# Inverses of the gated delta rule: five of six doubling levels in packed 32x32 blocks on four row groups

## The chip, the cores and the metric

One core of a Trainium2 chip runs one program of about thirty stages. The metric is the device time of one execution in microseconds (us). The program's tiles stay in the core's SBUF and PSUM; weights come over DMA. TensorE (PE) multiplies, VectorE (DVE), ScalarE (ACT) and GpSimd (POOL) do the elementwise work.

## The reference, cut to what matters

The stage in question makes, for each of 8 heads and each of 8 chunks of 64 tokens, the inverse of a unit lower triangular 64x64 matrix, in float32:

```python
k_beta = k * beta[..., None]
lmat = jnp.where(strict, jnp.einsum('bhncd,bhnsd->bhncs', k_beta, k) * decay, 0.0)
eye = jnp.eye(CHUNK, dtype=jnp.float32)
t_inv = lax.linalg.triangular_solve(eye + lmat, jnp.broadcast_to(eye, lmat.shape),
                                    left_side=True, lower=True, unit_diagonal=True)
u = jnp.einsum('bhncs,bhnsd->bhncd', t_inv, v_beta)
w = jnp.einsum('bhncs,bhnsd->bhncd', t_inv, k_beta * jnp.exp(g)[..., None])
```

The kernel works on chunks of 128 tokens (two of the reference's chunks and the block that joins them), so that 4 chunks cover the 512 tokens, and inverts 128x128 unit triangular matrices.

## The kernel before, in words

`gdn_inverse` (L1216 to L1350) is one stage. `gdn_layer` calls it twice, for heads 0 to 3 and for heads 4 to 7; the four heads of a call are worked on side by side. Every stage ends in a barrier of all engines (L175), so nothing of the next stage runs beside it.

The inverse is built by doubling. A head's matrix is kept as two diagonal blocks of 64x64 per chunk, the upper one on partitions 0 to 63 (`low`) and the lower one on 64 to 127 (`high`): `am` holds the strict triangle, `pair` the inverse found so far (4 chunks x 64 columns) and its transpose (4 chunks x 64 columns more). Each of six levels doubles the size b of the inverted diagonal blocks, from 1 to 64, with T <- T - T (A masked) T, in five steps for each head i (n = 4*level + i counts them through):

1. POOL multiplies `am` by the level's mask into one of two buffers `part` (L1252, 128x256). From n = 2 on it waits until `u` of n-2 has been issued, since that frees the buffer.
2. PE makes `u` = masked A times T in PSUM: 8 matmuls of 64x64, alternating between the low and the high row group (L1276). It waits for the cut of n (and, from level 1 on, for the head's last update).
3. DVE scales `u` by beta into `prod` (L1323, 128x256).
4. PE makes `p`: 16 matmuls of 64x64 (L1288 for T's half, L1289 for the transposed half), chunk by chunk, low and high.
5. DVE subtracts `p` from `pair` (L1334, 128x512).

PE's order is written out: in each level `u` of the four heads, then `p` of the four heads. After six levels each 128x128 matrix lacks the block that joins its halves: one head after the other has 4+4 matmuls on one row group each (L1301, L1307), a scaling by DVE (L1323, 64x256) and a copy by ACT (L1349), and ACT copies the finished halves to the full matrices `inv_t` (L1346).

Beside that, the stage begins with DVE's four copies of the identity into `pair` (L1314, 128x512) and two large matmuls whose result nobody reads, which keep PE busy (L194, called by `keep_busy`), and POOL zeroes `inv_t` after its second cut (L1256, 128x2048), makes the scaled keys `kb` in the last levels (L1259, four of 128x512) and scales `k_tok` behind its last cut (L1263, four of 128x512). The masks of the levels lie in `gdn_masks`, 7 x 64 columns, loaded once in the program's first stage.

A float32 matmul of the code stands in the trace as two weight loads and two matmul records, four instructions of PE.

Of the kernel before, what the change touches and what calls it, by code (L numbers as in the profile page):

```python
# [26 lines left out]
P = 128  # L27
# [12 lines left out]
NCH = S // CH  # L40
LEVELS = 7
HB = CH // 2
HG = 4

FF_PART = 1408
# [1170 lines left out]
def gdn_inverse(prog, name, h0, beta, am, pair, inv_t, prod, part, k_tok, beG, kd, kb):  # L1216

    nc, ps = prog.nc, prog.ps
    DEEP = LEVELS - 1
    N = DEEP * HG
    W = NCH * HB
    low, high = slice(0, HB), slice(HB, P)

    def blocks(x):
        return x.rearrange("p (c n) -> p c n", n=HB)  # L1230

    def cut_of(c):
        return slice(c * HB, (c + 1) * HB)
    part = part[:, :, 0:W]
    hs = slice(h0 * P, (h0 + HG) * P)

    def heads(x):
        return x.rearrange("p (h n) -> p h n", n=P)
    eye = prog.level_masks[:, DEEP, :]
    with Stage(prog, name) as st:  # L1240
        start, cut, cleared = st.counter("start"), st.counter("cut"), st.counter("cleared")
        u_ready, u_copied = st.counter("u_ready"), st.counter("u_copied")
        p_ready, updated = st.counter("p_ready"), st.counter("updated")
        corner_ready, placed, keyed = st.counter("corner_ready"), st.counter("placed"), st.counter("keyed")

        @st.gpsimd
        def _(pool):
            for n in range(N):
                level, i = divmod(n, HG)
                if n >= 2:  # L1250
                    pool.wait_ge(u_ready, n - 1)
                nc.gpsimd.tensor_tensor(blocks(part[:, n % 2, :]), blocks(am[:, i, 0:W]),  # L1252
                                        prog.level_masks[:, level, :].unsqueeze(1).to_broadcast([P, NCH, HB]),
                                        ALU.mult).then_inc(cut, 1)
                if n == 1:
                    nc.gpsimd.memset(inv_t[:, :, :], 0.0).then_inc(cleared, 1)  # L1256
                if n >= N - 2 * NCH and n % 2:
                    c = (n - (N - 2 * NCH)) // 2
                    nc.gpsimd.tensor_tensor(heads(kb[:, c, :]), heads(k_tok[:, c, hs]),  # L1259
                                            beG[:, c, h0:h0 + HG].unsqueeze(2).to_broadcast([P, HG, P]), ALU.mult).then_inc(keyed, 1)  # L1260
            for c in range(NCH):
                pool.wait_ge(keyed, c + 1)
                nc.gpsimd.tensor_tensor(heads(k_tok[:, c, hs]), heads(k_tok[:, c, hs]),  # L1263
                                        kd[:, c, h0:h0 + HG].unsqueeze(2).to_broadcast([P, HG, P]), ALU.mult)

        @st.tensor
        def _(pe):
            def u(n):
                i = n % HG
                pe.wait_ge(cut, n + 1)  # L1270
                pe.wait_ge(start, min(n + 1, HG))
                if n >= HG:
                    pe.wait_ge(updated, n - HG + 1)
                for c in range(NCH):
                    for rows in (low, high):
                        m = nc.tensor.matmul(ps[rows, i, cut_of(c)], part[rows, n % 2, cut_of(c)],  # L1276
                                             pair[rows, i, cut_of(c)], start=True, stop=True)
                m.then_inc(u_ready, 1)

            def p(n):  # L1280
                i = n % HG
                pe.wait_ge(u_copied, n + 1)
                if n >= HG:
                    pe.wait_ge(updated, n - HG + 1)
# [8 lines left out]
            for level in range(DEEP):  # L1293
                for i in range(HG):
                    u(level * HG + i)
                for i in range(HG):
                    p(level * HG + i)
# [12 lines left out]

        @st.vector
        def _(dve):
            for i in range(HG):
                m = nc.vector.tensor_copy(blocks(pair[:, i, :]), eye.unsqueeze(1).to_broadcast([P, 2 * NCH, HB]))  # L1314
                m.then_inc(start, 1)

            def scaled(n, rows):
# [4 lines left out]
                scale = beta[rows, :, h0 + i:h0 + i + 1].to_broadcast([rows.stop - rows.start, NCH, HB])  # L1322
                nc.vector.tensor_tensor(blocks(prod[rows, i, 0:W]), blocks(ps[rows, i, 0:W]), scale, ALU.mult  # L1323
                                        ).then_inc(u_copied, 1)
            for level in range(DEEP):
                for i in range(HG):
                    scaled(level * HG + i, slice(0, P))
                for i in range(HG):
                    n = level * HG + i
                    dve.wait_ge(start, HG)  # L1330
                    if n >= HG:
                        dve.wait_ge(updated, n - HG + 1)
                    dve.wait_ge(p_ready, n + 1)
                    nc.vector.tensor_tensor(pair[:, i, :], pair[:, i, :], ps[:, HG + i, :], ALU.subtract).then_inc(updated, 1)  # L1334
            for i in range(HG):
                scaled(N + i, high)

        @st.scalar
        def _(act):
            def full(i, rows):  # L1340
                return inv_t[rows, i, :].rearrange("p (c n) -> p c n", n=P)
            act.wait_ge(cleared, 1)
# [265 lines left out]
def gdn_layer(prog, inp):  # L1608
    nc = prog.nc
    with ExitStack() as own:  # L1610
# [10 lines left out]
        masks = new("gdn_masks", [P, LEVELS * HB])  # L1621
        prog.level_masks = masks[:, :].rearrange("p (l n) -> p l n", n=HB)
        with ExitStack() as mid:
            q, k, z = (new(n, s, mid) for n, s in (("gdn_q", [P, HEADS, S]), ("gdn_k", [P, HEADS, S]), ("gdn_z", [P, NT, D])))
            with ExitStack() as before:
# [2 lines left out]
            with ExitStack() as early:  # L1628
# [2 lines left out]
                ba = new("gdn_ba", [P, NT, 2 * HEADS], early)  # L1631
                sums = new("gdn_sums", [P, NT * 2 * HEADS], early)
                first_stage(prog, inp, [(taps[:, :], inp["gdn_taps"]), (par[:, :], inp["gdn_par"]),
                                        (masks[:, :], inp["cst"][:, 3 * P:3 * P + LEVELS * HB])])
# [2941 lines left out]
def constants():  # L4576
# [3 lines left out]
    ones = np.ones((P, P))  # L4580
    tri = (i[:, None] <= i[None, :]) * 1.0
    levels = []
    s, c = i[:, None] % HB, i[None, 0:HB]
    for level in range(LEVELS - 1):
        b = 1 << level
        levels.append((s // (2 * b) == c // (2 * b)) & (s % (2 * b) < b) & (c % (2 * b) >= b))
    levels.append(s == c)
    return np.concatenate([ident, ones, tri] + [m * 1.0 for m in levels], axis=1).astype(np.float32)

# [87 lines left out]
```

## Time and profile before

| | |
|---|---|
| device time, median of 3 runs | 2674.49 us (2668.77 to 2674.54) |
| the profiled execution, its own time | 2675.39 us |
| its span in the trace | 2673.7 us |
| mean granted TensorE clock, share of full speed | 0.983 |
| PE busy over the span | 94% |
| first call of `gdn_inverse` | 244.0 to 290.5 us of the span |
| second call | 334.1 to 380.5 us |

### The profile page before, as it was taken

To read this page: it belongs to the slowest core of one execution; us is meant where nothing else is said; L and a number is where in the kernel's file an instruction comes from. 1 tells how busy PE (TensorE), PEld (TensorE's weight loads), DVE (VectorE), ACT (ScalarE), POOL (GpSimd) and SP (SyncE) were. 2 spreads that over 40 slices of the span, in tenths; PEclk is the share of its full clock that TensorE was granted. 3 is DMA by queue.
4 is the path that set the end of the run, shared out by engine and by line. 5 is a ranking of instruction groups with operands and counts; after the bars stand their busy time and mean duration, and the time that the engine had idled before them with its cause. 6 is when DMAs were issued, how large, how long until landed. Compare 5 with 4: busy or idle time off the path is not lost. (4 is left out here: it accounts for less than half of the span.)

```text
span 2673.7 us, 41986 instructions
## 1 busy us (share of the span) xinstructions
PE 2526.5 (94%) x16381; PEld 2079.4 (78%) x16381; DVE 1721.1 (64%) x2858; ACT 1032.3 (39%) x1475; POOL 545.4 (20%) x429
## 2 busy tenths in 40 slices
PE   8998989999999989899999999989998989999897
PEld 7887887788887769799999999957774666776466
DVE  6745666467667773667676667755785546677456
ACT  3341213421212342455555555513343443344353
POOL 1104441430320200234233334410110001020001
PEclk9999999999999999899999999999999999999999
DMA  4220001347653442367777767743220212222021
GB/s 150 91 83 33 2 3 63 129 151 249 199 190 119 132 108 64 123 224 251 233 234 251 237 228 245 264 135 93 77 81 27 85 56 78 90 83 66 27 79 63
DMA packets 262241, 340.80 MB, mean 127 GB/s; under 512 B 24960, under 2 KB 220032, under 8 KB 261504
## 3 DMA queue, kind: packets, MB, share of 16 engines
q1 hardware_dynamic: 253888, 315.52, 36.4%
q0 software_dynamic: 4736, 16.78, 1.8%
q10 hardware_dynamic: 3456, 6.29, 0.8%
q8 instruction: 109, 1.79, 0.3%
q14 instruction: 52, 0.43, 0.1%
HBM read 318.63 MB, written 17.30 MB: 126 GB/s over the span
## 5 line engine op out<-in xcount | busy, mean ns | idle before, releaser
L2946 PE MATMUL ps<-x_feat_r,moe_w_hi 128*128 128x384 f32 x1408 | 405.1, 359 | 1.0 <-DVE x_feat_r L3046 1.0
L2511 DVE TENSOR_TENSOR moe_w_lo<-ring,moe_w_hi 128x2048 fp32r<-128x2048 f32 x144 | 315.8, 2193 | 118.8 <-ACT moe_w_hi L2506 118.8
L2949 PE MATMUL ps<-x_feat_r,moe_w_lo 128*128 128x192 f32 x1408 | 354.5, 252 | 0.0
L2506 ACT ACTIVATE moe_w_hi<-ring 128x2048 fp32r<-128x2048 f32 x144 | 254.8, 1770 | 93.0 <-PE ps L263 75.5
L2949 PEld LDWEIGHTS ps<-x_feat_r,moe_w_lo 128*128 128x128 f32 x1408 | 268.8, 191 | 0.3
L2946 PEld LDWEIGHTS ps<-x_feat_r,moe_w_hi 128*128 128x128 f32 x1408 | 264.3, 188 | 1.9 <-issue 1.6
L267 PE MATMUL ps<-x_free_r,ring_r 128*128 128x512 f32 x496 | 196.5, 396 | 0.0
L266 PE MATMUL ps<-ring_r,x_feat_r 128*128 128x256 f32 (+2 forms) x576 | 186.3, 323 | 0.0
L194 PE MATMUL ps<-cst 128*128 128x384 f32 x326 | 125.8, 538 | 21.0 <-PEq L175 19.0
L263 PE MATMUL ps<-x_feat_r,ffn_w_hi 128*128 128x512 f32 x352 | 139.3, 396 | 1.2 <-DVE ffn_w_lo L2454 1.2
L267 PE MATMUL ps<-x_feat_r,ffn_w_lo 128*128 128x512 f32 x352 | 139.4, 396 | 0.0
L266 PE MATMUL ps<-x_free_r,ffn_w_hi 128*128 128x512 f32 x352 | 138.5, 393 | 0.0
L2506 ACT ACTIVATE ffn_w_hi<-ring 128x2048 fp32r<-128x2048 f32 (+1 forms) x35 | 61.8, 1768 | 170.1 <-PE ps L263 101.0
L3854 ACT ACTIVATE s_sb<-s_sb,att_small 128x512 f32<-128x512 f32 (+3 forms) x128 | 71.8, 561 | 140.7 <-DVE att_small L3846 140.3
L266 PEld LDWEIGHTS ps<-ring_r,x_feat_r 128*128 128x128 f32 x576 | 110.5, 192 | 8.7 <-issue 0.6
L194 PEld LDWEIGHTS ps<-cst 128*128 128x128 f32 x326 | 65.6, 209 | 66.2 <-issue 34.8
L267 PEld LDWEIGHTS ps<-x_free_r,ring_r 128*128 128x128 f32 x496 | 93.7, 189 | 21.1
L3843 DVE CUSTOM_DVE_ANT_0 s_sb<-ps,tables 128x128 f32<-128x128 f32 (+3 forms) x104 | 49.3, 474 | 94.0 <-PE ps L3793 75.2
L3861 ACT ACTIVATE p_t<-ps 128x512 f32<-128x512 f32 (+3 forms) x128 | 55.1, 431 | 132.0 <-PE ps L3793 132.0
L263 PE MATMUL ps<-x_feat_r,acc_r 128*128 128x512 f32 x256 | 102.3, 400 | 0.0
L2993 ACT ACTIVATE moe_cross<-ps 128x384 f32<-128x384 f32 (+1 forms) x96 | 44.4, 463 | 148.2 <-PE ps L2949 148.2
L267 PE MATMUL ps<-x_feat_r,ring_r 128*128 128x512 f32 x256 | 101.1, 395 | 0.0
(619 smaller groups left out, 6455.3 us busy)
## 6 DMA issues: line engine op xcount, KB each, us to landing
ring<-in_moe_w SPq DMA_DIRECT2D x120, 1024.0 KB, 5.3
ring<-in_w_in SPq DMA_DIRECT2D x32, 1024.0 KB, 5.3
ring<-in_ffn_w SPq DMA_DIRECT2D x30, 1024.0 KB, 7.6
ring<-in_ada_t SPq DMA_DIRECT2D x48, 512.0 KB, 4.0
ring<-in_gdn_w_in SPq DMA_DIRECT2D x12, 1024.0 KB, 5.7
ring<-in_moe_w SPq DMA_DIRECT2D x24, 512.0 KB, 3.7
ring<-in_s_w_glu SPq DMA_DIRECT2D x8, 1024.0 KB, 5.6
ring<-in_w_out SPq DMA_DIRECT2D x8, 1024.0 KB, 6.4
```

Of the source, the lines that this page charges most:

```text
L194: prog.nc.tensor.matmul(prog.ps[:, bank, 0:3 * P], prog.ident, prog.cst, start=True, stop=True)
L263: m = nc.tensor.matmul(out, lh, rh, start=first, stop=False)
L266: nc.tensor.matmul(out, lh, rl, start=False, stop=False)
L267: return nc.tensor.matmul(out, ll, rh, start=False, stop=last)
L2506: self.prog.nc.scalar.activation(self.flat(self.hi, j % SPLITS, j), self.raw(j), ACT.Copy).then_inc(self.hi_done, 1)
L2511: self.prog.nc.vector.tensor_tensor(self.flat(self.lo, j % SPLITS, j), self.raw(j), self.flat(self.hi, j % SPLITS, j).bitcast(F32), ALU.su ...
L2946: mm = nc.tensor.matmul(out, wh[:, k, cs], both[:, k, :], start=(k == 0), stop=False)
L2949: mm = nc.tensor.matmul(out[:, 0:SLOTS], wl[:, k, cs], xg[0][:, k, :], start=False, stop=(k == KD - 1))
L2993: nc.scalar.activation(cross_of(c, which), half(c, which, 1), ACT.Copy).then_inc(cross_copied, 1)
L3843: self.nc.vector.tensor_tensor_reduce(out=x, in0=scores, in1=table, scale=1.0, scalar=-3.0e38, op0=ALU.add, op1=ALU.max, accum_out=mx).the ...
L3854: self.nc.scalar.activation(x, x, ACT.Exp, bias=self.small[:, u % 4, 1:2], scale=self.heads[h][3], accum_out=self.small[:, u % 4, 2:3]).th ...
L3861: self.nc.scalar.activation(self.p_t[:, u % 2, 0:self.keys(u)], self.ps[:, 2 + u % 2, 0:self.keys(u)], ACT.Copy).then_inc(self.pt_copied, 1)
```

## The change

Levels 0 to 4 now work on 32x32 blocks. For them the chunk's four 32x32 diagonal blocks lie on four row groups (partitions 0 to 31, 32 to 63, ...), and a head's operands are packed to 4 chunks x 32 columns:

- `am_small` is `am` without the columns that belong to the other block of a pair, packed at the stage's start by two copies on ACT (L1415) and two on DVE (L1362), 32x4x128 each. POOL waits for all four.
- A level's `u` is 16 matmuls of 32x32 for a head (L1293), its `p` 32 (L1306, L1309), four row groups in turn. DVE scales 128x128 (L1370) and subtracts 128x256 (L1386) for a head, POOL's cut is 128x128 (L1274).
- Level 0 multiplies by the identity from the mask table instead of `pair`; `p` there is 16 matmuls for a head, and DVE makes both halves of the pair as identity minus a product (L1379, L1381). The four copies L1314 are gone.
- After level 4 the pair is widened to the old form for the last level: two copies on DVE (L1391, L1392) and two on ACT (L1426, L1427) for a head, 32x8x32 each, into `pair`, which POOL has zeroed after its fourth cut (L1281). The last level (L1321, L1331, L1332) waits for them (`wide_act`, `wide_dve`); it and the joining blocks (L1348, L1354) are as before.
- The key scalings leave POOL and stand on ACT, 16 + 16 instructions of 128x128 (L1411). ACT also zeroes the lower left blocks of `inv_t` (L1419, four of 64x256) in place of POOL's memset of the whole.
- The mask table is 256 columns in place of 448. The stage's semaphore counters are 14 in place of 10.

In matmuls of the code a call has 608 before (24 x 8 for `u`, 24 x 16 for `p`, 32 at the end), and 1024 after (128 in level 0, 192 in each of levels 1 to 4, 96 in the last level, 32 at the end).

```diff
+            pool.wait_ge(packed_act, 2)
+            pool.wait_ge(packed_dve, 2)
             for n in range(N):
                 level, i = divmod(n, HG)
                 if n >= 2:
                     pool.wait_ge(u_ready, n - 1)
...
+                if n < NQ:
+                    nc.gpsimd.tensor_tensor(blocks(part[:, n % 2, 0:QW], QB), blocks(am_small[:, i, :], QB),
+                                            prog.quarter_masks[:, level, :].unsqueeze(1).to_broadcast([P, NCH, QB]),
+                                            ALU.mult).then_inc(cut, 1)
...
+            def u_quarters(n):
+                i = n % HG
+                pe.wait_ge(cut, n + 1)
+                if n >= HG:
+                    pe.wait_ge(updated, n - HG + 1)
+                for c in range(NCH):
+                    cs = cut_of(c, QB)
+                    for rows in quarters:
+                        m = nc.tensor.matmul(ps[rows, i, cs], part[rows, n % 2, cs],
+                                             pair_small[rows, i, cs] if n >= HG else eye[rows], start=True, stop=True)
+                m.then_inc(u_ready, 1)
+
+            def p_quarters(n):
...
+                for c in range(NCH):
+                    cs, ts = cut_of(c, QB), cut_of(NCH + c, QB)
+                    if n >= HG:
+                        for rows in quarters:
+                            nc.tensor.matmul(ps[rows, HG + i, cs], pair_small[rows, i, ts], u_small[rows, i, cs],
+                                             start=True, stop=True)
+                    for rows in quarters:
+                        m = nc.tensor.matmul(ps[rows, HG + i, ts], u_small[rows, i, cs],
+                                             pair_small[rows, i, ts] if n >= HG else eye[rows], start=True, stop=True)
+                m.then_inc(p_ready, 1)
...
-            for i in range(HG):
-                m = nc.vector.tensor_copy(blocks(pair[:, i, :]), eye.unsqueeze(1).to_broadcast([P, 2 * NCH, HB]))
-                m.then_inc(start, 1)
...
+                    if level == Q_LEVELS - 1:
+                        dve.wait_ge(updated, n + 1)
+                        dve.wait_ge(emptied, 1)
+                        nc.vector.tensor_copy(*widen(i, 2))
+                        nc.vector.tensor_copy(*widen(i, 3)).then_inc(wide_dve, 1)
```

What it does to the order of the engines, at three places. PE's own list, the first two levels of a call, before (one of its four heads' `p`, each row a matmul of the code or several alike):

```order
L194 MATMUL ps<-cst 128x384 x2
L1276 MATMUL ps<-gdn_inv,gdn_sq 64x64 x32
L1288 MATMUL ps<-x_feat,gdn_inv 64x64
L1289 MATMUL ps<-gdn_inv,x_feat 64x64
L1288 MATMUL ps<-x_feat,gdn_inv 64x64
L1289 MATMUL ps<-gdn_inv,x_feat 64x64
```

and the same place after:

```order
L197 MATMUL ps<-cst 128x384 x2
L1293 MATMUL ps<-gdn_masks,gdn_sq 32x32 x64
L1309 MATMUL ps<-gdn_masks,x_feat 32x32 x64
L1293 MATMUL ps<-x_feat,gdn_sq 32x32 x64
L1306 MATMUL ps<-x_feat 32x32 x4
L1309 MATMUL ps<-x_feat 32x32 x4
```

The order of `u` and `p` is kept; a level has twice as many matmuls, of a quarter of the block each, and level 0 has no L1306.

DVE's list around the last two levels of a call, where `x_feat` is the packed `prod` and `gdn_inv` the `pair`, before (three last levels, and the scalings at the end):

```order
L1323 TENSOR_TENSOR x_feat<-ps,gdn_small 128x256 x4
L1334 TENSOR_TENSOR gdn_inv<-gdn_inv,ps 128x512 x4
L1323 TENSOR_TENSOR x_feat<-ps,gdn_small 128x256 x4
L1334 TENSOR_TENSOR gdn_inv<-gdn_inv,ps 128x512 x4
L1323 TENSOR_TENSOR x_feat<-ps,gdn_small 64x256 x4
```

and after (level 4 with one head's widening, of which four stand there, and the last level):

```order
L1370 TENSOR_TENSOR x_feat<-ps,gdn_small 128x128 x4
L1386 TENSOR_TENSOR x_feat<-x_feat,ps 128x256
L1391 COPY gdn_inv<-x_feat 32x8x32
L1392 COPY gdn_inv<-x_feat 32x8x32
L1386 TENSOR_TENSOR x_feat<-x_feat,ps 128x256
...
L1370 TENSOR_TENSOR x_feat<-ps,gdn_small 128x256 x4
L1399 TENSOR_TENSOR gdn_inv<-gdn_inv,ps 128x512 x4
```

The copies stand between the subtractions of level 4, ahead of the last level's scalings.

POOL's list of a call, before:

```order
L1252 TENSOR_TENSOR gdn_sq<-x_free,gdn_masks 128x256 x2
L1256 MEMSET x_free 128x2048
L1252 TENSOR_TENSOR gdn_sq<-x_free,gdn_masks 128x256 x16
L1259 TENSOR_TENSOR acc<-gdn_ktok,gdn_small 128x512
L1252 TENSOR_TENSOR gdn_sq<-x_free,gdn_masks 128x256 x2
```

and after:

```order
L1274 TENSOR_TENSOR gdn_sq<-x_feat,gdn_masks 128x128 x4
L1281 MEMSET gdn_inv 128x2048
L1274 TENSOR_TENSOR gdn_sq<-x_feat,gdn_masks 128x128 x16
L1278 TENSOR_TENSOR gdn_sq<-x_free,gdn_masks 128x256 x4
```

The memset has moved from behind the second cut to behind the fourth, the cuts are half as wide, and no key scaling is left.

## Rows read from the trace of the kernel before

**Rows 1.** The span by stretches of stages: length, busy time with records, clock, DMA.
```profile
core 0: us, PE busy (x) PEld busy (x) DVE busy (x) ACT busy (x) POOL busy (x), PEclk, DMA share, GB/s
244.00:292.00 48.00, 44.84 (x1232) 41.44 (x1233) 31.57 (x57) 4.83 (x12) 26.88 (x33) 0.96 0.02 4
334.00:382.00 48.00, 43.19 (x1233) 40.58 (x1234) 32.02 (x57) 4.83 (x12) 27.14 (x33) 1.00 0.02 4
```

**Rows 2.** Marks in time of the first call: barrier, first u, first corner block.
```profile
L175 PEldq EVENT_SEMAPHORE x2: 51/51/51, 244.0 to 290.5; - x2
...
L1276 PE MATMUL ps<-gdn_inv,gdn_sq x384: 218/218/366, 246.9 to 282.5; 64*64 64x64 f32 x192
...
L1301 PE MATMUL ps<-gdn_inv,x_free x32: 218/218/267, 286.1 to 288.0; 64*64 64x64 f32 x32
```

**Rows 3.** Groups of instructions in 244 to 292: count, busy us, mean ns, idle before.
```profile
L1252 POOL TENSOR_TENSOR gdn_sq<-x_free,gdn_masks 128x256 f32<-128x256 f32 x24 | 17.2, 737 | 16.4 <-PE ps L1276 15.5 <-POOLq L175 0.3
L1334 DVE TENSOR_TENSOR gdn_inv<-gdn_inv,ps 128x512 f32<-128x512 f32 x24 | 16.5, 687 | 8.3 <-PE ps L1289 8.3
L1276 PE MATMUL ps<-gdn_inv,gdn_sq 64*64 64x64 f32 x384 | 15.6, 226 | 2.4 <-POOL gdn_sq L1252 2.3
L1323 DVE TENSOR_TENSOR x_feat<-ps,gdn_small 128x256 f32<-128x256 f32 x24 | 9.7, 420 | 5.0 <-PE ps L1276 5.0
L1259 POOL TENSOR_TENSOR acc<-gdn_ktok,gdn_small 128x512 f32<-128x512 f32 x4 | 4.2, 1040 | 0.0
L1346 ACT ACTIVATE x_free<-gdn_inv 64x256 f32<-64x256 f32 x8 | 3.3, 415 | 43.7 <-DVE gdn_inv L1334 43.5
```

**Rows 4.** One level of the first call, by stretches: its p phase, its u phase.
```profile
256.60:260.34 3.74, 3.74 (x135) 3.74 (x133) 2.34 (x5) 0.00 (x0) 1.04 (x2) 1.00 0.02 4
260.34:263.08 2.74, 2.34 (x72) 2.07 (x70) 1.93 (x5) 0.00 (x0) 1.78 (x3) 1.00 0.00 0
```

**Rows 5.** Records on one row group alone, and L2322's first loads after idle time.
```profile
L1307 PE MATMUL ps<-gdn_inv,x_feat x32: 218/218/267, 287.8 to 289.7; 64*64 64x64 f32 x32
...
961.60:961.64 0.04, 0.01 (x1) 0.04 (x2) 0.50 0.00 0
```

**Rows 6.** DMA queues in 244 to 290, and in 250.2 to 253.8 with its 40 slices.
```profile
q8 instruction: 10, 0.16, 1.5%
...
DMA  0700000000000000000000000000000000000007
q8 instruction: 2, 0.03, 3.8%
```

**Rows 7.** A far jump of PE's sequencer, then DMA in 1762.5:1765.1, 1765.1:1765.8, 1765.8:1767.
```profile
L3220 PEldq COMPARE_BRANCH  x2: 89/1829/3569, 1109.1 to 1761.5; - x2
...
q8 instruction: 1, 0.02, 3.0%
...
DMA packets 0, 0.00 MB, mean 0 GB/s; under 512 B 0, under 2 KB 0, under 8 KB 0
...
q8 instruction: 1, 0.02, 5.0%
```

**Rows 8.** Stretches ahead of a lower granted clock, and at it (columns as in rows 1).
```profile
224.30:227.70 3.40, 1.47 (x14) 1.24 (x13) 1.30 (x4) 1.91 (x4) 1.95 (x2) 0.99 0.00 0
227.70:231.10 3.40, 3.40 (x18) 3.40 (x18) 3.24 (x8) 0.29 (x1) 2.86 (x2) 0.51 0.02 5
237.90:241.30 3.40, 1.16 (x9) 0.86 (x8) 1.18 (x3) 2.20 (x4) 2.35 (x2) 1.00 0.01 2
241.30:244.70 3.40, 0.62 (x1) 0.50 (x2) 2.80 (x6) 0.00 (x0) 3.08 (x3) 0.50 0.00 0
```

**Rows 9.** Nearest rows for the new small operations, from other stages of the program.
```profile
L3861 ACT ACTIVATE p_t<-ps 128x128 f32<-128x128 f32 x32 | 8.7, 272 | 29.2 <-PE ps L3793 29.2
L3854 ACT ACTIVATE s_sb<-s_sb,att_small 128x128 f32<-128x128 f32 x32 | 12.8, 401 | 29.8 <-DVE att_small L3846 29.6
L3874 DVE COPY acc<-ps 128x128 f32<-128x128 f32 x64 | 18.2, 284 | 10.9 <-PE ps L3808 10.9
```

More of the change, by code:

```diff
@@ L1223, in gdn_inverse, with blocks, cut_of, side @@
     nc, ps = prog.nc, prog.ps
-    DEEP = LEVELS - 1
-    N = DEEP * HG
-    W = NCH * HB
+    N = (Q_LEVELS + 1) * HG
+    NQ = Q_LEVELS * HG
+    W, QW = NCH * HB, NCH * QB
     low, high = slice(0, HB), slice(HB, P)
[L1229 to L1233, printed above, removed]
+    quarters = [slice(r * QB, (r + 1) * QB) for r in range(P // QB)]
+    def blocks(x, n=HB):
+        return x.rearrange("p (c n) -> p c n", n=n)
+    def cut_of(c, n=HB):
+        return slice(c * n, (c + 1) * n)
+    def side(r):
+        return slice((r % 2) * QB, (r % 2 + 1) * QB)
     part = part[:, :, 0:W]
     hs = slice(h0 * P, (h0 + HG) * P)
+    u_small, am_small, pair_small = prod[:, :, 0:QW], prod[:, :, QW:2 * QW], prod[:, :, 2 * QW:4 * QW]
     def heads(x):
         return x.rearrange("p (h n) -> p h n", n=P)
-    eye = prog.level_masks[:, DEEP, :]
+    eye = prog.quarter_masks[:, Q_LEVELS, :]
     with Stage(prog, name) as st:
-        start, cut, cleared = st.counter("start"), st.counter("cut"), st.counter("cleared")
+        cut, cleared, emptied = st.counter("cut"), st.counter("cleared"), st.counter("emptied")
+        packed_act, packed_dve = st.counter("packed_act"), st.counter("packed_dve")
+        wide_act, wide_dve = st.counter("wide_act"), st.counter("wide_dve")
         u_ready, u_copied = st.counter("u_ready"), st.counter("u_copied")
@@ L1251, in _ @@
                     pool.wait_ge(u_ready, n - 1)
[L1252 to L1264, printed above, removed]
+                if n < NQ:
+                    nc.gpsimd.tensor_tensor(blocks(part[:, n % 2, 0:QW], QB), blocks(am_small[:, i, :], QB),
+                                            prog.quarter_masks[:, level, :].unsqueeze(1).to_broadcast([P, NCH, QB]),
+                                            ALU.mult).then_inc(cut, 1)
+                else:
+                    nc.gpsimd.tensor_tensor(blocks(part[:, n % 2, :]), blocks(am[:, i, 0:W]),
+                                            prog.half_mask.unsqueeze(1).to_broadcast([P, NCH, HB]), ALU.mult).then_inc(cut, 1)
@@ L1292, in _ @@
             keep_busy(prog, 2 * HG - 1, 2)
-            for level in range(DEEP):
+            for level in range(Q_LEVELS):
                 for i in range(HG):
-                    u(level * HG + i)
+                    u_quarters(level * HG + i)
                 for i in range(HG):
-                    p(level * HG + i)
+                    p_quarters(level * HG + i)
+            for i in range(HG):
+                u(NQ + i)
+            for i in range(HG):
+                p(NQ + i)
             for i in range(HG):
@@ L1312, in _, with scaled @@
         def _(dve):
-            for i in range(HG):
-                m = nc.vector.tensor_copy(blocks(pair[:, i, :]), eye.unsqueeze(1).to_broadcast([P, 2 * NCH, HB]))
-                m.then_inc(start, 1)
-            def scaled(n, rows):
+            eyes = eye.unsqueeze(1).to_broadcast([P, NCH, QB])
+            for r in (2, 3):
+                nc.vector.tensor_copy(*pack(r)).then_inc(packed_dve, 1)
+            def scaled(n, rows, width=HB):
                 i = n % HG
@@ L1321, in scaled @@
                     dve.wait_ge(p_ready, n - HG + 1)
[L1322 to L1325, printed above, removed]
+                scale = beta[rows, :, h0 + i:h0 + i + 1].to_broadcast([rows.stop - rows.start, NCH, width])
+                nc.vector.tensor_tensor(blocks(prod[rows, i, 0:NCH * width], width), blocks(ps[rows, i, 0:NCH * width], width),
+                                        scale, ALU.mult).then_inc(u_copied, 1)
@@ L1335, in _ @@
+            for i in range(HG):
+                scaled(NQ + i, slice(0, P))
+            for i in range(HG):
+                dve.wait_ge(wide_act, i + 1)
+                dve.wait_ge(wide_dve, i + 1)
+                dve.wait_ge(p_ready, NQ + i + 1)
+                nc.vector.tensor_tensor(pair[:, i, :], pair[:, i, :], ps[:, HG + i, :], ALU.subtract).then_inc(updated, 1)
             for i in range(HG):
@@ L1341, in full, with scale_keys @@
                 return inv_t[rows, i, :].rearrange("p (c n) -> p c n", n=P)
+            def scale_keys(dst, factor):
+                for c in range(NCH):
+                    for h in range(HG):
+                        m = nc.scalar.activation(heads(dst[:, c])[:, h, :], heads(k_tok[:, c, hs])[:, h, :], ACT.Copy,
+                                                 scale=factor[:, c, h0 + h:h0 + h + 1])
+                return m
+            for r in (0, 1):
+                nc.scalar.activation(*pack(r), ACT.Copy).then_inc(packed_act, 1)
+            scale_keys(kb, beG).then_inc(keyed, 1)
+            nothing = prog.ones[high, 0:1].unsqueeze(2).to_broadcast([HB, NCH, HB])
+            for i in range(HG):
+                m = nc.scalar.activation(full(i, high)[:, :, low], nothing, ACT.Copy, scale=0.0)
+            m.then_inc(cleared, 1)
+            act.wait_ge(keyed, 1)
+            scale_keys(k_tok[:, :, hs], kd)
+            act.wait_ge(emptied, 1)
+            for i in range(HG):
+                act.wait_ge(updated, NQ - HG + i + 1)
+                nc.scalar.activation(*widen(i, 0), ACT.Copy)
+                nc.scalar.activation(*widen(i, 1), ACT.Copy).then_inc(wide_act, 1)
             act.wait_ge(cleared, 1)
@@ L4582, in constants @@
     levels = []
-    s, c = i[:, None] % HB, i[None, 0:HB]
-    for level in range(LEVELS - 1):
+    s, c = i[:, None] % QB, i[None, 0:QB]
+    for level in range(Q_LEVELS):
         b = 1 << level
```

50 lines of the change are left out of this document (37 added, 13 removed).

## Prediction

> **What bounds the kernel now.** I read the busy shares by stretches first. The two calls of the stage take 46.4 us each (barrier at 244.0, next at 290.5 [rows 2]), together 3.5% of the span; PE is busy for 93% and 90% of them, DVE for some 66%, and DMA moves next to nothing (share 0.02) [rows 1]. No transfer runs underneath that a shorter stage would expose, and each stage ends in a barrier, so what the stage gains or loses I pass on whole, twice. The profiled execution took 2675.39 us against a median of 2674.49; I add differences to the median.
>
> Inside a call, the marks in time give three parts [rows 2]: 2.9 us until the first u, 39.2 us of six levels, 4.4 us of corner blocks. One level is 3.74 us of p, in which PE is never idle, and 2.74 us of u, in which PE waits for POOL's cuts [rows 4]; 6.48 us together. A float32 matmul of the code is four PE instructions, so p's 64 matmuls in 3.74 us are 58.4 ns each, 29.2 ns per matmul record, 14.6 ns per instruction. One row group alone takes 1.9 us for 31 intervals of a record, 61 ns each [rows 5]: two row groups really ran side by side, and the rate of p is that of the array. That is what the change attacks.
>
> **The change, part by part.** I divide a call after the change into a fixed part and Q, the time of the five narrow levels.
>
> Start. POOL's first cut now waits for packing. The nearest row for the copy is ACT at 415 ns for 64x256 [rows 3]; for twice the columns I take 0.6, then about 0.35 to hand over, 0.45 for a cut of half the elements of the 737 ns one [rows 3], and the rest of the start-up: 1.75 us until the first u, in place of 2.9. (In the second call it was 1.5; I keep 1.75 for both.)
>
> Last level: 6.5 us as a level of before [rows 4]. Corner: 4.3. Widening: DVE has two copies more for each head between subtractions. The bounds are 284 ns (a 128x128 copy [rows 9]) and ACT's 415 [rows 3]; four heads are about 2.2 us more on DVE, of which the next head's p hides most. I charge 1.0 us, with 0 to 2.5 as the ends. Fixed part: 1.75 + 1.0 + 6.5 + 4.3 = 13.55 us. The call breaks even at Q = 46.35 − 13.55 = 32.8 us.
>
> Moved off POOL: 8.2 us of key scalings (L1259 four times 1.04, and four like it) [rows 3]. They lay in POOL's gaps or behind its last cut; on ACT they are 32 instructions of 272 to 401 ns [rows 9], 9 to 13 us, where ACT was idle for 43.7 us [rows 3]. Widening is wanted some 25 us or more after the start, so I cost this at nothing; without that cover it would be those 9 to 13 us. The memset behind cut 3 is 1.8 us of POOL in a level whose cuts have shrunk to about 0.45; it may hold up level 1's first cuts by about a microsecond, once. POOL's waits (2.3 us of PE's idle time [rows 3]) shrink with the cuts. The shorter mask table belongs to the program's first stage and is hidden: nothing.
>
> Q, if PE and DVE alone decide. A level has 192 matmuls of 32x32 on four row groups. If a group needs about as long as it does for 64 columns now (61 ns per record at the most [rows 5], half of that with the half-wide block), a matmul costs 61/4, about 15.6 ns, and a level 3.0 us of PE. DVE then has four scalings and four subtractions of half the size (9.7 us and 16.5 us for 24 of each now [rows 3], so 2.2 us a level at half the elements), with the latency from PE to DVE and back at both seams: 3.7 us a level. Level 0 has 128 matmuls and eight instructions on DVE, 3.8. Q = 3.8 + 4 x 3.7 = 18.6, and a call takes 32.2, 14.2 us less.
>
> But PE has to get its instructions. A narrow level is 768 of them, and a block of 256 would be used up in 1.0 us. On the instruction queue there are 10 packets of 16 KB in 46 us [rows 6], and PE had about 2465 records in the stage [rows 1], so one packet is 256 instructions. They come one at a time: two within 250.2 to 253.8, one at either end, and none between [rows 6], 3.5 us apart, just as fast as PE uses them up. A packet takes 16 x 46 x 1.5% / 10 = 1.10 us. How far ahead is it asked for? The far jump at 1761.5 shows it [rows 7]: the branch lasts 3.57 us, until 1765.07; the target's packet takes 1.25 us of it (3.0% of 16 x 2.6); from 1765.1 to 1765.8 no packet of any kind moves; at 1765.8, 0.75 us after PE went on, the next block's packet begins. So the next block is asked for when the engine enters the one ahead of it, and not before. From entering a block to being able to enter the next it takes L = 0.75 + 1.10, and what it takes from the packet's end until its instructions can be used. The jump shows 1.3 us for that. The ends: 1.85 us (nothing behind the packet) and 3.4 (the whole branch, less the longer packet: 3.57 − 1.25 + 1.10). I take 3.15, since only the jump shows the steps one by one. Before, a block lasted at least 3.74 us in the p phase, so none of this could be seen.
>
> The narrow levels have 128 + 4 x 192 = 896 matmuls, 3584 instructions, 14 blocks. The first is there; 13 are waited for: Q = 1.0 + 13 x 3.15 = 42.0. A call takes 55.5 us, 9.2 more than now; two calls **+18.3 us**. At L = 1.85 it would be Q = 25.1, 38.6 us, −15.4 for both; at 3.4, +24.8; the change breaks even at L = 2.45.
>
> The page "Runtime: NRT & Kernel Launch" of the Trainium skill, section Instruction fetch mechanics, also has blocks of 256 instructions, the next fetched while the current one runs, and calls crossing into one "mostly hidden". With that in the narrow levels the call would take the 32.2 us worked out above; the trace agrees on the size of a block, and is silent on whether one of 1.0 us can hide a packet.
>
> **Clock.** A PE that works 1.0 us in 3.15 is idle for most of the time. The granted clock fell to 0.50 behind stretches with PE busy for 1.47 and 1.16 of 3.4 us, and stayed there for at least 3.4 us [rows 8]. While PE waits for instructions that costs nothing; at the entry into the last level, 3.4 us of work at half clock lose 1.7 us. Twice: +3.4. With it 2674.5 + 18.3 + 3.4 = 2696; since it may have risen again by then, I write 2695.
>
> **The rivals.**
> (1) *Fetch is hidden* (more than one block ahead once the stream is sequential). Then Q is set by PE and DVE: 18.6 us, total −28.4, 2646; if the front of PE is slower than the array, less is won. After idle time the next load followed within 40 ns of the first [rows 5]; taken as the price of a matmul's four instructions, 896 of them are 35.8 us, with 1 us of waits Q = 36.8, +8. The case spans 2646 to 2682, the low end likelier, since that row is a bound from above. For it: nothing before ever ran short. Against it: the 0.7 us without a packet after the jump [rows 7].
> (2) *Fetch binds, but quicker*: L from 1.85 to 2.6. 2659 to 2678.
> (3) *Slower by issue, whatever is fetched*: PE never got past one matmul record in 29.2 ns or an instruction in 14.6 ns [rows 4]. If that is the limit of the front and not of the array, a level is 192 x 58.4 = 11.2 us and level 0 7.5: Q = 52.4, 66 us a call, +39 in all, 2714. It turns the sum from about 35.5 ns a matmul on (31.8 us over 896). Against it: one row group alone takes 61 ns per record [rows 5], two together half of that, as an array limit would have it.
> The page "TensorE: Matmul & The Clock Gate", section Wait — 56ns, not 53.3ns?, has start-to-start never under about 25 ns, however small the matmul. Taken across row groups, two records a matmul, that is an estimate of 50 ns, 9.6 us a level, Q = 45, +24; the 29.2 ns of rows 4 do not contradict it.
> (4) *The change doesn't do what it says*: were the four groups not run side by side, a level would be as in (3) or worse; it goes into its chance.
>
> **How the numbers follow.** Forecast (fetch-bound, L 2.6 to 3.4): 0.40, 2679 to 2704. Rival 1: 0.27. Rival 2: 0.18. Rivals 3 and 4: 0.15, 2698 to 2714. What a measurement of this kernel can tell from no change is 0.3%, 8 us. Faster by more: four fifths of rival 1 and half of rival 2, 0.31. Within: the rest of both, and a tenth of the forecast (its short end), 0.18. Slower by more: 0.51. The range leaves the fastest end of rival 1 and the upper end of rival 3 out: 2650 to 2706.
>
> **What would show it.** In the trace of after: packets on the instruction queue in the narrow levels at a steady distance L whatever PE does, with all engines idle between the end of one block's work and the next; the first u at about 1.75 us; a narrow level of 9 to 10 us; the clock at 0.50 in places; DVE's share of the stage down. If packets come 1.0 to 1.3 us apart, rival 1 holds; if PE's records are evenly spaced by about 29 ns through the narrow levels, rival 3. My forecast falls if more than one block is in store.

## The result, and the profile after

The changed kernel takes 2714.8 us (median of 4 runs, 2714.1 to 2715.5) against 2674.5 us (2668.8 to 2678.6): a ratio of 1.0147, 95% interval 1.0135 to 1.0159, 40.3 us more. The forecast was 2695 us, range 2650 to 2706: the sign was right, the size half of what came. All times in this document are of fast runs alone, which leaves out one of five runs of the kernel called "both" below, at 4937 us.

All of it lies in the two calls. First the barriers at either end of both, then both calls by stretch (length, busy time with records of PE, PEld, DVE, ACT, POOL, the granted clock, DMA share), of the changed kernel:

```profile
L178 PEldq EVENT_SEMAPHORE  x2: 51/51/51, 246.2 to 312.8; - x2
L178 PEldq EVENT_SEMAPHORE  x2: 51/51/51, 356.4 to 422.4; - x2
...
246.15:312.83 66.68, 41.45 (x2052) 37.01 (x2052) 22.91 (x66) 20.30 (x58) 13.54 (x25) 0.61 0.02 4
356.36:422.39 66.03, 41.10 (x2052) 36.58 (x2052) 23.17 (x66) 20.30 (x58) 13.53 (x25) 0.61 0.02 4
```

A call was 46.4 us [rows 2] and is 66.7 and 66.0 now: 40 us together. PE has 820 records more on either side than before [rows 1], and yet is busy for fewer microseconds: 41.5 of 66.7 in the first call. DVE and POOL, most of whose instructions were halved in size, are busy for less as well. By the records of all engines, none of them works for 27% of the first call and 24% of the second, and for a third of the narrow levels. The granted clock, 0.96 and 1.00 before, is 0.61.

What ended PE's idle time, from the groups of instructions in 244 to 310 (busy us, mean ns, then the idle time ahead and its releaser):

```profile
L1309 PE MATMUL ps<-x_feat 32*32 32x32 f32 x512 | 15.8, 236 | 7.2 <-issue 7.2
L1306 PE MATMUL ps<-x_feat 32*32 32x32 f32 x512 | 15.7, 236 | 7.3 <-issue 7.3
L1293 PE MATMUL ps<-x_feat,gdn_sq 32*32 32x32 f32 x512 | 9.0, 226 | 8.6 <-issue 7.8 <-POOL gdn_sq L1274 0.8
```

"issue" is time in which the engine waited for nothing that the profile shows: no semaphore, no other engine. The three rows have 22.3 us of it together. Before, no row of this stage had more than 1.1 us of it in the levels; the idle time of L1276 was POOL's [rows 3].

What it was stands in four stretches of level 1 and the start of level 2 (in pairs: PE working, PE stopped), and in the DMA of 261 to 268 (40 slices of 0.175 us):

```profile
260.00:261.75 1.75, 1.72 (x127) 1.71 (x127) 0.74 (x2) 0.00 (x0) 0.00 (x0) 0.50 0.03 9
261.75:264.00 2.25, 0.23 (x16) 0.10 (x8) 0.10 (x1) 0.00 (x0) 0.00 (x0) 0.50 0.00 0
264.00:265.75 1.75, 1.73 (x127) 1.73 (x126) 0.75 (x2) 0.00 (x0) 0.00 (x0) 0.50 0.04 9
265.75:267.85 2.10, 0.19 (x14) 0.06 (x5) 0.32 (x2) 0.00 (x0) 0.45 (x1) 0.50 0.00 0
...
DMA  0000300000000000000000004000000000000000
q8 instruction: 2, 0.03, 2.0%
```

PE runs 127 matmul records and as many loads, one block of 256 instructions, in 1.75 us; then hardly anything runs on the whole core for 2.1 to 2.3 us, and the next 127 follow. The packet with the next block starts at 261.7 and 265.3, near the end of each burst (a burst is such a run of 256 instructions), and the burst that it feeds begins 2.3 to 2.6 us later. Over the narrow levels it goes on like that:

```profile
DMA packets 13, 0.21 MB, mean 4 GB/s; under 512 B 0, under 2 KB 0, under 8 KB 0
q8 instruction: 13, 0.21, 2.0%
```

13 packets in 250 to 300, 3.83 us apart in the mean, 3.45 to 4.12 each; a packet itself takes 16 x 50 x 2.0% / 13 = 1.2 us.

The last level, its u and its p:

```profile
300.50:304.40 3.90, 3.79 (x68) 3.53 (x65) 2.61 (x8) 1.43 (x4) 1.54 (x2) 0.50 0.02 4
304.40:308.40 4.00, 4.00 (x128) 4.00 (x126) 2.10 (x4) 1.08 (x3) 0.00 (x0) 0.89 0.03 6
```

7.9 us against the 6.48 of [rows 4]: u at half clock, p at nearly full.

### The profile page after: what moved, and what is told of

It is laid out like the page before. It is cut to its first block and busy times, and to the rows that moved or that the text cites. A ratio compares the mean times of both kernels' runs of the same rounds, so it can differ in the third digit from the quotient of the medians.

```text
span 2713.8 us, 45414 instructions
## 1 busy us (share of the span) xinstructions
PE 2522.2 (93%) x18045; PEld 2071.8 (76%) x18045; DVE 1703.8 (63%) x2878; ACT 1063.5 (39%) x1567; POOL 518.3 (19%) x413
## 5 line engine op out<-in xcount | busy, mean ns | idle before, releaser
L197 PEld LDWEIGHTS ps<-cst 128*128 128x128 f32 x326 | 64.2, 205 | 64.0 <-issue 31.8
```

The source lines that it names most:

```text
L197: prog.nc.tensor.matmul(prog.ps[:, bank, 0:3 * P], prog.ident, prog.cst, start=True, stop=True)
```

## The experiments

### Ten stages of PE work alone

Two explanations give almost the same time for this kernel: waiting for blocks of instructions (13 x 3.8 us), and a PE that cannot issue faster than 14.6 ns per instruction (rival 3, which came out at 2714). The trace shows bursts, which speak for the first; this kernel holds everything else away.

```diff
+def probe(prog, name, size, groups, n, loop):
+    rows = [slice(r * size, (r + 1) * size) for r in range(groups)]
+    def work(count):
+        for j in range(count // groups):
+            bank, at = (j // 2) % 7, (j % 2) * P
+            for r in rows:
+                nc.tensor.matmul(ps[r, bank, at:at + n], prog.ident[r, 0:size], prog.cst[r, 0:n], start=True, stop=True)
...
+            if loop:
+                with pe.Fori(0, loop):
+                    work(64)
+            else:
+                work(384)
```

> The kernel before with ten more stages ahead of the first call of gdn_inverse, each with PE work alone, whose results nobody reads: 384 matmuls written out (stages a, b, c: 32x32 blocks on four row groups with 32, 64, 128 moving columns; h: 64x64 blocks on two row groups with 64 columns) or a loop of 12 rounds of 64 matmuls (d, e, f: as a, b, c; g: as h; i and j: 32x32 blocks with 32 columns on one and on two row groups). Each starts with the same 12 large matmuls. Fetch theory (a block of 256 PE instructions follows the one ahead by about 3.9 us at the least, as the trace of the changed kernel has it): a, b and c take the same time, six blocks of 3.9 us, some 23 us, whatever the columns; d, the same matmuls twice over in a loop that fetches nothing after its first round, takes 768 times 15 to 27 ns, 12 to 21 us, and e and f take more with the columns. Issue theory (PE takes about 15 ns for each of its instructions, four a matmul): a takes 384 x 58 ns = 22 us as well, but d takes 768 x 58 ns = 45 us. g should take 58.4 ns a matmul in both, 45 us, and h 22 us: there no fetch shows. i tells what one row group takes: if d's time a matmul is a quarter of it, the array sets d.

The ten stretches a to j, in order (length first; a matmul of the code is two records):

```profile
256.65:275.98 19.33, 10.20 (x769) 9.55 (x768) 0.00 (x0) 0.00 (x0) 0.00 (x0) 0.61 0.02 5
287.26:306.01 18.75, 11.83 (x769) 11.19 (x768) 0.00 (x0) 0.00 (x0) 0.00 (x0) 0.98 0.02 4
317.67:339.81 22.14, 21.70 (x768) 20.89 (x768) 0.00 (x0) 0.00 (x0) 0.00 (x0) 1.00 0.01 4
348.73:365.27 16.54, 15.24 (x1536) 14.01 (x1536) 0.00 (x0) 0.00 (x0) 0.00 (x0) 1.00 0.00 1
374.17:397.37 23.20, 23.20 (x1537) 21.88 (x1536) 0.00 (x0) 0.00 (x0) 0.00 (x0) 1.00 0.00 1
406.23:448.09 41.86, 41.86 (x1537) 41.85 (x1536) 0.00 (x0) 0.00 (x0) 0.00 (x0) 1.00 0.00 0
457.01:501.80 44.79, 44.79 (x1536) 44.79 (x1536) 0.00 (x0) 0.00 (x0) 0.00 (x0) 1.00 0.00 0
510.67:533.07 22.40, 22.40 (x769) 22.40 (x768) 0.00 (x0) 0.00 (x0) 0.00 (x0) 1.00 0.01 4
541.93:619.88 77.95, 77.95 (x1536) 77.95 (x1536) 0.00 (x0) 0.00 (x0) 0.00 (x0) 0.54 0.00 0
631.59:656.94 25.35, 25.35 (x1537) 25.15 (x1536) 0.00 (x0) 0.00 (x0) 0.00 (x0) 1.00 0.00 1
```

a and d are the same matmul, 32x32 with 32 columns on four row groups. Written out, 384 of them take 19.3 us, 50.3 ns each, with PE busy for half of it; in a loop, 768 take 16.5 us, 21.5 ns each. So PE issues an instruction in 5.4 ns or less: rival 3 has fallen, and so has the prediction's estimate of 50 ns for a matmul. Written out, twice the columns (b) cost nothing, 18.8 us (b began with more of its list at hand, 526 records ahead of its first stop against 324 in a, but its bursts lie 3.7 to 4.0 us apart and those of a 3.5 to 3.7), and four times the columns (c) 3 us more than a; in a loop the same steps cost 16.5, 23.2 and 41.9 us (21.5, 30.2, 54.5 ns a matmul). The 64x64 form takes 58.3 ns whether written out (h) or in a loop (g): 256 of its instructions last 3.7 us, and a packet is on its way meanwhile. Six blocks had been expected to take some 23 us; a and b took 19, since only four or five of their blocks were waited for. The packets of a lay 3.33 to 3.79 us apart (mean 3.62, at a clock of 0.61), those of b 3.49 to 4.12 (mean 3.82, at 0.98): the interval is no shorter at the higher clock.

What several row groups bring has to be compared at one clock. Stage i, on one row group, ran at full clock only at its start; the granted clock then fell to 0.50, though PE was never idle in it:

```profile
541.93:545.00 3.07, 3.07 (x98) 3.07 (x98) 0.00 (x0) 0.00 (x0) 0.00 (x0) 1.00 0.02 5
550.00:560.00 10.00, 10.00 (x192) 10.00 (x191) 0.00 (x0) 0.00 (x0) 0.00 (x0) 0.50 0.00 0
```

At 1.00 its matmul records start 31.8 ns apart, 64 ns a matmul; two row groups (j) take 33.0 and four (d) 21.5. So the second row group halves the time and the third and fourth together take another third off. A quarter of one group's time would be 16 ns; what keeps four groups at 21.5 stays open.

### The narrow levels in a loop

If the waits are for fetching, PE's list must be shortened without taking a matmul away. In this kernel the five narrow levels are five rounds of one loop on PE; the other engines are as in the changed kernel, but for level 0, which is like the others and has 64 matmuls more.

```diff
-            for level in range(Q_LEVELS):
+            with pe.Fori(0, Q_LEVELS) as e:
                 for i in range(HG):
-                    u_quarters(level * HG + i)
+                    u_quarters(i, e)
                 for i in range(HG):
-                    p_quarters(level * HG + i)
+                    p_quarters(i, e)
...
+            def gate(i):
+                nc.tensor.matmul(ps[0:HB, i, BANK - 1:BANK], prog.ident[0:QB, 0:HB], prog.cst[0:QB, 0:1], start=True, stop=True)
```

> The changed kernel with its five narrow levels on PE in a hardware loop of five rounds, so that their 768 instructions are fetched once and not five times. Level 0 is then like the others (192 matmuls, the pair begins as copies of the identity), and ahead of each head's u and p stands one matmul with a single moving column that carries the wait. Matmuls of the narrow levels: 960 + 40 in place of 896. Fetch theory: three blocks of 3.9 us once, then four levels at PE's own rate (15 to 27 ns a matmul, 3.7 to 6 us a level): Q of 27 to 36 us in place of 52, so 32 to 50 us less in all than the changed kernel, 2665 to 2683 us. Issue theory (58 ns a matmul): no gain, 2715 us or a little more.

2702.0 us (ratio to before 1.0109, 1.0092 to 1.0126): 13 us less than the changed kernel, not 32 to 50. The fetching did go, and something else took its place. Two levels of it:

```profile
265.00:274.00 9.00, 8.81 (x420) 8.14 (x412) 2.85 (x8) 0.00 (x0) 1.81 (x4) 0.50 0.00 0
274.00:283.00 9.00, 8.77 (x416) 8.10 (x412) 2.85 (x8) 0.00 (x0) 1.81 (x4) 0.50 0.00 0
```

PE is busy for 98% of it, and a level takes 9.0 us. The cost was my own gate: a head's 16 matmuls of u took 0.42 us, and the next head's began 0.88 us after the first of them, so a gate took 0.46 us at half clock, and a level has eight. So the gate was put on PE's sequencer:

```diff
             def gate(i):
-                nc.tensor.matmul(ps[0:HB, i, BANK - 1:BANK], prog.ident[0:QB, 0:HB], prog.cst[0:QB, 0:1], start=True, stop=True)
+                pe.sem_inc(passed, 1)
```

> As loop5 (the five narrow levels in a hardware loop on PE), but the eight waits of a level stand on a semaphore instruction of PE's sequencer in place of a small matmul over two column groups. In loop5 four heads' u started 0.88 us apart with 0.42 us of matmuls in each, at half clock. If those matmuls were what ate the gain, a level goes from 9.0 us to 5.0 + the two seams between PE and DVE of 0.5 us, some 6 us at half clock and 4.5 at full clock: 11.7 + 4 x 6 = 36 us for the narrow levels, 50 to 53 us a call in place of 60, 2681 to 2687 us. If the levels are held up by something else (PE to DVE and back, POOL), it stays near 2700.

2672.4 us (median of 10; ratio to before 0.9988, 0.9979 to 0.9997), 9 us below the range expected. The first four of the five levels, in order:

```profile
247.43:256.06 8.63, 4.71 (x385) 4.26 (x385) 2.67 (x8) 8.58 (x30) 3.45 (x5) 0.90 0.02 6
256.06:262.09 6.03, 5.57 (x384) 5.37 (x385) 2.67 (x9) 0.76 (x3) 1.75 (x4) 0.50 0.00 0
262.09:267.02 4.93, 4.14 (x384) 3.94 (x385) 3.05 (x9) 0.00 (x0) 1.74 (x4) 0.95 0.00 0
267.02:271.75 4.73, 4.04 (x385) 3.84 (x385) 2.81 (x9) 0.00 (x0) 1.74 (x4) 1.00 0.00 0
...
q8 instruction: 3, 0.05, 0.6%
```

Three packets in 247 to 276, where the changed kernel has 13 in 247 to 300. The first round waits for its blocks (8.6 us), the second takes 6.0 us at half clock, the later ones 4.7 to 4.9 us at full clock, for 192 matmuls. Against the changed kernel's 11.5 us a level (three blocks of 3.83) even the round at half clock is half as long, so it was the fetching and not the clock that made the level long. With the fetching of four rounds taken away, 64 matmuls a call more and the clock that came with it, the kernel is 42 us faster than the changed one, more than the whole loss against before. The clock rose at the third level. That PE ran without long gaps by then isn't the whole reason: in the kernel with the small matmuls PE was busy for 98% of these levels and the clock stayed at 0.50 through all of them. What raises it isn't shown.

### Filling PE to hold the clock

```diff
                 pe.sem_inc(passed, 1)
+                if i == 0:
+                    nc.tensor.matmul(ps[:, i, BANK // 2:BANK], prog.ident, prog.cst[:, 0:BANK // 2], start=True, stop=True)
```

> As loop5e with one 128x128 matmul of 256 columns ahead of each level's u and each level's p, whose result nobody reads: ten a call, 0.3 us each at full clock, 3 us a call. If the low granted clock of the narrow levels comes from PE doing too little in them, these keep it at 1.00, a matmul of a narrow level costs 16 to 21 ns in place of 26, and a level 4.5 us; 48 us a call, 2677 us. If the clock stays at 0.50, they cost 5 us a call and the time is 10 us above that of loop5e.

2682.3 us, 10 us above loop5e. It reads like the case in which the clock stays low, but it isn't: here are 30 us of either call.

```profile
250.00:280.00 30.00, 24.45 (x1553) 20.01 (x1551) 11.13 (x32) 6.10 (x20) 8.02 (x18) 0.83 0.00 1
350.00:380.00 30.00, 25.09 (x1588) 20.60 (x1588) 12.60 (x37) 4.31 (x14) 7.50 (x16) 0.83 0.00 1
```

The rounds at full clock start 6.1 us apart in place of 4.7 to 4.9: a filler costs some 0.65 us, not 0.3. That is its own work: like every float32 matmul it is two matmul records, here 0.32 us apart, and the packed matmuls go on 0.31 us after the second. I had priced one record for two. The run therefore says nothing about what a steady clock would be worth.

### Two narrow levels in place of five

```diff
-Q_LEVELS = LEVELS - 2
+Q_LEVELS = 2
+WIDE_LEVELS = LEVELS - 1 - Q_LEVELS
```

with the masks of the other four levels in 64x64 form, and these levels run in it.

> The changed kernel with two narrow levels in place of five; levels 2 to 5 run in 64x64 blocks as before, and widening stands behind level 1. Fetch or issue theory alike: a narrow level is three blocks of 3.9 us, 11.7 to 11.9 us, a wide one 6.5; three levels fewer in the narrow form are 3 x 5.3 = 16 us a call less, 32 in all, 2683 us. If it were instead something that comes once in a call (the packing, the widening, the clock at the end), the time would stay within 5 us of 2715.

2683.8 us (1.0031, 1.0018 to 1.0044), as forecast to the microsecond: 31 us less than the changed kernel for three levels fewer in each of two calls, 5.2 us a level. Both explanations had forecast this, so it doesn't part them. The loss is a price per narrow level; packing, widening and the start can hold a few microseconds of it at most.

### The key scalings back on POOL

The changed kernel, with L1411's 32 instructions gone from ACT and the four plus four of before on POOL again.

> The changed kernel with one part undone: the key scalings are on POOL again, between the last eight cuts and behind them. The prediction costed the move at nothing. PE waits 2 us and more for each block of instructions in levels 3 and 4, so POOL's four operations of 1.04 us there are covered; in the last level PE is the slower. Expected: 2715 us, within 3. If POOL's scalings were on the path, up to 4 us a call more, 2723.

2708.7 us, under the 2712 to 2718 expected, but its four runs spread over 2702.7 to 2715.6. It isn't slower than the changed kernel (2714.1 to 2715.5), so moving the keys had brought nothing that shows. Whether it is faster isn't settled: the ratios to before, 1.0137 (1.0120 to 1.0154) and 1.0147 (1.0135 to 1.0159), overlap. Its profiled run was its fastest, with a span 13 us shorter than that of the changed kernel's profiled run, and only 3.8 us of them lie within the two calls. The packets lay 3.70 and 3.77 us apart in its two calls, against 3.83 and 3.76, which explains 1.5 us.

### The good parts without the narrow blocks

Two things in the stage need no 32x32 block: level 0 from the identity (a part of the change), and PE's waits for POOL's cuts [rows 3, 4], which four buffers end (2.3 us of PE's idle time in the first call before, none with four buffers). `part` is twice as wide as its two buffers, so the room is there.

```diff
-    part = part[:, :, 0:W]
+    part = part.rearrange("p b (a n) -> p (b a) n", n=W)
...
-                if n >= 2:
-                    pool.wait_ge(u_ready, n - 1)
+                if n >= HG:
+                    pool.wait_ge(u_ready, n - HG + 1)
...
-                                             pair[rows, i, cut_of(c)], start=True, stop=True)
+                                             pair[rows, i, cut_of(c)] if n >= HG else eye[rows], start=True, stop=True)
```

Both together:

> The kernel before, in 64x64 blocks throughout, with two parts of its own: level 0 multiplies by the identity from the mask table and leaves out its product for the first half (32 matmuls fewer, no copies of the identity at the start), and POOL's cuts go through four buffers in place of two. In level 0 1.9 us of p go, and up to 1.5 us of the start; the waits of PE for POOL's cuts, 0.9 us in each of five levels, go as well: 6 to 7 us a call less than before, 2661 to 2663 us. If the waits for POOL only move to another place, half of that, 2668.

Both, with the key scalings on ACT:

> As wide_both (64x64 blocks, first level from the identity, four buffers for the cuts), with the key scalings moved from POOL to ACT as in the changed kernel and POOL's memset behind the fourth cut. POOL's 1.04 us operations between the last cuts held nobody up once the cuts ran ahead by four buffers: no change against wide_both, 2665 us, within 2 us. If they still delayed cuts, up to 1 us a call less. Against the kernel before: 9 us less, 0.3 to 0.4%.

Level 0 from the identity alone:

> The kernel before with one part of the change alone, in 64x64 blocks: level 0 multiplies by the identity from the mask table, leaves out the product for the first half (32 matmuls of 58.4 ns, 1.9 us) and the copies of the identity at the start. The last of these held PE up in both calls (first u at 2.9 and 1.5 us, second head's at 4.9 and 3.8 us). Expected 2 to 3.5 us a call less, 2667 to 2670 us. If the waits for POOL's cuts take the gain away, 1 us a call, 2672.

Four buffers alone:

> The kernel before with four buffers for POOL's cuts in place of two, and nothing else. PE's waits for the cuts, 0.9 us in each of five levels, go, and POOL's 24 cuts of 0.74 us (18 us a call) stay below PE's time: 3 to 4.5 us a call less, 2666 to 2669 us. The two single changes together should come to the 9 us of the combined kernel.

| kernel | us | ratio to before, 95% |
|---|---|---|
| level 0 from the identity alone | 2668.3 | 0.9982 (0.9971 to 0.9994) |
| four buffers alone | 2667.2 | 0.9971 (0.9959 to 0.9982) |
| both | 2663.4 | 0.9954 (0.9938 to 0.9970) |
| both, key scalings on ACT | 2661.4 | 0.9957 (0.9945 to 0.9969) |

The last two are one result by their ratios. The barriers of a call of the third, and the first call of the fourth by stretch:

```profile
L175 PEldq EVENT_SEMAPHORE  x2: 51/51/51, 243.9 to 285.7; - x2
...
244.38:285.92 41.54, 40.26 (x1156) 37.52 (x1156) 27.80 (x56) 14.40 (x44) 19.14 (x25) 0.96 0.02 4
```

41.8 and 41.5 us for a call in place of 46.4, PE busy for 97% of the latter. Both beat the kernel before and the changed one, by 0.4% and by 2%. Each single change came in within its expectation; the two gains add up, 0.18% and 0.29% alone and 0.46% together, at the short end of what was expected.

With the waits for POOL gone, blocks of instructions begin to be waited for in the 64x64 form too. With four buffers alone, first call:

```profile
PEld ps L1288 <- issue: 0.5, 2, 0.3
```

Both stops lie within a level's p, where the kernel before has none, and each ends 1.3 us after a packet's end (265.4 and 280.7, packets until 264.1 and 279.4), which is what it takes between the bursts of the changed kernel. It costs little as yet, but little more can be won here while PE's list is written out.

## Why the prediction was right and wrong

**What bounds the changed stage: right.** The forecast named the block of 256 instructions, asked for only when the engine enters the one ahead; the steady packets, the idle core between the bursts and the low clock are there, and the two loops (stage d and the narrow levels) show that the waiting goes when nothing has to be fetched. The sign followed.

**The term that failed: L.** The prediction put 3.15 us between two blocks and closed its bounds at 3.4; the trace has 3.83 in the mean. Over the narrow levels of the first call the three pieces of L = 0.75 + 1.10 + 1.3 measure 1.24 + 1.20 + 1.40: from a block's first matmul to the start of the next block's packet, the packet, and from its end to the next burst. The second and the third piece were 0.1 us short each; the first, 0.5 us short, is the one that failed. After the jump the packet had begun 0.75 us after PE went on [rows 7]; between the bursts it begins 1.0 to 1.7 us after a block's first matmul. I had one jump and took its smallest step for a constant, and had made the upper bound from the same jump. What the asking waits for in that time stays open; it was not shorter at full clock (1.1 to 1.7 us in stage b). The rows of before held a hint that I didn't use: the two packets of 250.2 to 253.8 [rows 6] were about 3.5 us apart. That is no lower bound for L, since PE used its instructions up no faster, but no row showed fetching to be any quicker than that. That it could be the slower of the two there, only just hidden, was not excluded, and the break-even at 2.45 us was far below both. With 3.83, Q = 1.0 + 13 x 3.83 = 50.8 us in place of 42.0: 17.6 us of the missing 20 for both calls; the start below is another 2.4.

Of the first call, piece by piece (predicted, measured): start 1.75, 2.9; narrow levels with widening 43.0, 51.4; last level 6.5 and 1.7 for the clock, 7.9; corner 4.3, 4.4.

**The start: wrong by 1.2 us.** Packing was ready in time (POOL's second cut ended at 248.5), but PE still had its two large matmuls to finish (until 249.1), at half clock:

```profile
246.26 2.90 PE L197 MATMUL ps<-cst 128*128 128x384 f32 x4 [3.09 <-PEq L178]
249.09 0.36 PEld L1293 LDWEIGHTS ps<-gdn_masks,gdn_sq 32*32 32x32 f32 x20 [1.08 <-POOL gdn_sq L1274]
```

In the sum I replaced DVE's copies and left out the engine that had been the later one in the first call. The second call started in 2.9 us as well, its two large matmuls at half clock too (0.52), where before they had run at 1.00 and taken 1.5 us to the first u; what lowered the clock there isn't shown.

**The clock: right in size.** The last level took 1.4 us more in the first call, its u at 0.50; 1.7 were charged. That the low clock comes from the waiting is likely but not shown: it rose in one of the two loops and not in the other.

**The array: close.** The narrow matmul was put at 15.6 ns with an upper 40; in a loop without gates it takes 21.5 ns, a level 4.7 to 4.9 us at full clock and not 3.7. By an estimate from these (five levels at 1.1 us more) "fetch is hidden" would have brought about 9 us a call less, not 14: the gain was smaller than rival 1 said, even without its obstacle.

**Key scalings, cuts, memset at nothing: not contradicted.** L1411 ended at 258.5, the widening came at 296, and the key scalings put back on POOL made nothing slower. The memset was not tested alone.

**Rival 3 hit the number for the wrong reason.** It said 2714, 2714.8 was measured. 58.4 ns per matmul over a written-out list and 3.8 us per 256 instructions are the same rate; the busy share and the loop part them, the total doesn't.

## What to carry to other kernels

Cutting TensorE's work into smaller matmuls multiplies its instructions, and a list that is written out is read at no more than 256 instructions in some 3.8 us here, 15 ns each or 60 ns per float32 matmul: below that the size of a matmul is free, and only fewer instructions or a loop help. Before such a change, multiply the instructions by that figure and compare with the stage; look for the packets on the instruction queue, and for PE's idle time under "issue". And when PE waits for a helper's cut, more buffers for it may be worth more than faster arithmetic: here two more gave 7 us for five changed lines.

## What the runs showed of the hardware that I had not expected

- The interval of the blocks was 3.3 to 4.1 us in three kernels, at granted clocks from 0.5 to 1.00. In the 64x64 form 256 instructions last 3.7 us, so the kernel before ran at the edge of it without a trace of waiting. Over the six blocks of stage h it doesn't wait either; with four buffers for POOL, two blocks of the first call came a few tenths of a microsecond late.
- One row group alone takes 64 ns per float32 matmul of 32x32 with 32 columns at a clock of 1.00, two row groups 33.0 and four 21.5: the second brings more than the third and fourth together.
- The granted clock fell to 0.50 in stage i, with PE busy without a gap on one row group. In the kernel with the small matmuls it was 0.50 through the looped levels, with PE busy for 98%. A busy PE is thus no sign of a full clock: read the granted clock beside it.
- A matmul with a single moving column, over two column groups, between packed ones costs 0.46 us at half clock. With a semaphore instruction in its place no gap over 0.04 us shows between two heads' u, and a level at half clock takes 6.0 us in place of 9.0. In all it made 30 us of the kernel's time, with the clock, which stayed low in the one and rose in the other.
